# A two-layer encoder trunk on one core: the first projections run while the second half of x is still transposed and split

## What is computed

```python
def rms_norm(x, g):
    y = xf * lax.rsqrt(jnp.mean(xf * xf, axis=-1, keepdims=True) + EPS)
    return y * g
...
h = rms_norm(x, attn_norm_g[0])
qkv = h @ w_qkv                       # 1024 x 3072: q, k, v of 8 heads
q = rms_norm(q, q_g) * (A_HEAD_DIM ** -0.5)
k = rms_norm(k, k_g)
```

## Time and profile before

| | |
|---|---|
| median of 3 runs | 2355.66 us (2349.65 to 2358.06) |
| the profiled execution | 2355.31 us, its span 2353.6 us |
| TensorE busy | 2222.9 us, 94% |
| Vector engine busy | 1593.7 us, 68% |
| Scalar engine busy | 1162.1 us, 49% |
| GpSimd busy | 842.2 us, 36% |
| TensorE busy from 9.1 to 38 us | 15.95 us |
| first projection matmul | at 38.06 us |

### The profile page before, as it was taken

The page is one execution under the profiler, slowest core; times in us unless marked ns, Lnnn a source line. Parts: engine busy times, 40 slices in busy tenths (PEclk is TensorE's granted clock), DMA queues, the critical chain, the costliest instruction groups (busy, mean ns, idle before and its releaser), DMA issues.

```text
span 2353.6 us, 36507 instructions
## 1 busy us (share of the span) xinstructions
PE 2222.9 (94%) x11916; PEld 1909.4 (81%) x11916; DVE 1593.7 (68%) x3173; ACT 1162.1 (49%) x2483; POOL 842.2 (36%) x1464
## 2 busy tenths in 40 slices
PE   6999999976999999899999989998999999899998
PEld 5999999965878888788777988887878888778777
DVE  5688888763576666776776368875576666776773
ACT  4566666653455455533444256653455555543342
POOL 2333333343642222332334155554542233232331
PEclk9999999977999999999999899997999999999999
DMA  6111000002424444762452110003424444663352
GB/s 197 35 28 28 27 27 21 1 19 93 130 82 148 149 153 161 258 241 84 149 197 90 36 37 10 10 19 99 129 87 155 162 158 162 249 223 104 135 173 82
DMA packets 186756, 255.86 MB, mean 109 GB/s; under 512 B 15072, under 2 KB 135904, under 8 KB 181984
## 3 DMA queue, kind: packets, MB, share of 16 engines
q1 hardware_dynamic: 186592, 253.82, 32.3%
HBM read 174.09 MB, written 79.69 MB: 108 GB/s over the span
## 4 chain that ended last, share of the span: by engine, by line
PE 80%; DVE 10%; issue 5%; ACT 3%; DMA 1%; POOLq 1%; POOL 0%; DVEq 0%; SPq 0%; ACTq 0%
PE score L1855 45%; PE trb L1855 13%; PE proj L1855 13%; PE pv L1855 5%; DVE xop L1350 3%; DVE w_op L1350 1%; PE trb L2205 1%; PE trb L1893 1%; ACT p L960 1%; DVE xT L1591 1%; DVE p L1488 1%; DMA w_quad<-in_mlp_w_down 1%; DVE pb L1802 1%; ACT pb L1315 1%; PE trb L1945 0%
## 5 line engine op out<-in xcount | busy, mean ns | idle before, releaser
L1855 PE MATMUL score<-xop,w_op 128*128 128x512 f32 x3840 | 893.8, 392 | 25.3 <-DVE xop L1350 12.6
L1855 PEld LDWEIGHTS score<-xop,w_op 128*128 128x128 f32 x3840 | 720.8, 189 | 185.3 <-issue 36.1
L799 POOL TENSOR_TENSOR w_quad<-w_quad,w_sum 128x512 f32<-128x512 f32 x64 | 99.5, 1555 | 807.1 <-DVE w_op L1350 807.1
L1855 PE MATMUL trb<-xop,w_op 128*128 128x512 f32 x1536 | 361.9, 390 | 5.4 <-DVE w_op L1350 2.0
L1855 PEld LDWEIGHTS trb<-xop,w_op 128*128 128x128 f32 x1536 | 287.4, 188 | 68.8 <-issue 5.8
L923 ACT ACTIVATE w_op<-w_quad 128x512 fp32r<-128x512 f32 (+1 forms) x336 | 216.3, 645 | 247.0 <-PE score L1855 165.3
L1350 DVE TENSOR_TENSOR w_op<-w_quad,w_op 128x512 fp32r<-128x512 f32 (+1 forms) x336 | 285.0, 852 | 43.8 <-ACT w_op L923 43.8
L1591 DVE TENSOR_TENSOR xT<-score,xT 128x512 f32<-128x512 f32 x160 | 109.8, 686 | 159.0 <-PE score L1855 150.9
L1855 PE MATMUL score<-a_hi,w_op 128*128 128x512 f32 x512 | 162.1, 397 | 3.8 <-DVE w_op L1350 3.8
L960 ACT ACTIVATE p<-p,nm_a,slopes 128x128 f32<-128x128 f32 (+7 forms) x124 | 106.6, 861 | 112.6 <-DVE nm_a L1493 110.4
L1350 DVE TENSOR_TENSOR xop<-xop 128x1024 fp32r<-128x1024 f32 x112 | 143.3, 1290 | 16.3 <-ACT xop L923 16.3
(11 more groups left out here) (266 smaller groups left out, 4567.1 us busy)
## 6 DMA issues: line engine op xcount, KB each, us to landing
xop<-u_dram SPq DMA_DIRECT2D x112, 512.0 KB, 5.8
u_dram<-quad SPq DMA_DIRECT2D x32, 1536.0 KB, 9.7
w_quad<-in_mlp_w_up SPq DMA_DIRECT2D x64, 512.0 KB, 5.3
w_quad<-in_mlp_w_down SPq DMA_DIRECT2D x64, 512.0 KB, 4.9
wa_raw<-in_a_w_qkv SPq DMA_DIRECT2D x96, 128.0 KB, 2.4
quad<-xT_dram SPq DMA_DIRECT2D x32, 256.0 KB, 4.2
xT_dram<-xs SPq DMA_DIRECT2D x32, 256.0 KB, 2.6
u_dram<-quad SPq DMA_DIRECT2D x32, 256.0 KB, 4.0
```

Of the source, the lines that this page charges most:

```text
L799: return pool.tensor_tensor(out, x, y, ALU.subtract)
L1855: return nc.tensor.matmul(out, a, b, start=start, stop=stop, **kw)
```

## The change

1. x lies in two buffers of four blocks. The first stands where `v_parts` of both heads will be written, the second and one of the staging buffers in memory that nothing uses in the opening. The staging buffers (four) hold two units each, and one store takes both.
2. SyncE loads the first half of x, then the weights of head 0, then the second half of x. Stores and the loads of the small constants are issued in eight groups.
3. The units 0 to 7 (first half) are worked on with the four quarters of `wa_split` between them. The Scalar engine copies the even units to the staging buffer, the Vector engine the odd ones. The squares are shared: blocks 0, 1, 4, 5 on the Scalar engine, 2, 3, 6, 7 on the Vector engine.
4. The row factors are made by halves (`half_factors`).
5. TensorE runs block 0 as soon as its chunks and weights are there, and then transposes two units of the second half after each of the blocks 0 to 3. These units use two banks; blocks 2 and 3 go into the other two. Block 4 is the first that needs the second half.
6. The small products follow block 5, and only the first scores wait for lambda. The first quarter of the next head's weights is split at block 4 instead of 2.
7. The Scalar engine's function table is loaded by a copy of one column at the start.

```diff
@@ run_heads @@
-            head(-1, 1, False, False, True, True)
+            if first_head:
+                first_head()
+            else:
+                head(-1, 1, False, False, True, True)
@@ helpers @@
+        def x_bank(n):
+            if n < KC:
+                return bank[n % 2][n // 2 % 2]
+            return bank[0][n % 2]
+
         def qkv_bank(h, s):
+            if isinstance(h, int) and h < 0 and s in (2, 3):
+                return bank[1][s - 2]
             return pv if isinstance(h, int) and h < 0 and s % 2 == 0 else proj
@@ SyncE @@
+            load_x(0)
...
             for i in range(4):
                 load_wa(0, i)
+            load_x(1)
-            for n in range(2 * KC):
-                sp.wait_ge(x_staged, n + 1)
...
+            for n in range(0, 2 * KC, 2):
+                sp.wait_ge(x_staged, n // 2 + 1)
+                sp.wait_ge(x_staged_v, n // 2 + 1)
+                sp.dma_start(x_dram[:, n % KC:n % KC + 2, HALF * (n // KC):HALF * (n // KC + 1)],
+                             x_stage[n // 2 % 4][:, :, :]).then_inc(x_stored[n // 2 % 4], 16)
+                for dst, src in small[3 * (n // 2):3 * (n // 2) + 3]:
+                    col(dst, src, const_in)
@@ Scalar engine @@
+            act.wait_ge(made, 2)
+            copy(x_junk[0][:, 0:1], ones[:, 0:1])
+            def x_units(first, end):
+                for n in range(first, end):
+                    half, c = divmod(n, KC)
+                    act.wait_ge(x_tr, n + 1)
+                    copy(a_hi[:, c, HALF * half:HALF * (half + 1)], x_bank(n), gains[:, 0, c:c + 1]).then_inc(x_hi_done, 1)
+                    if n % 2 == 0:
+                        if n >= 8:
+                            act.wait_ge(x_stored[n // 2 % 4], 16)
+                        copy(x_stage[n // 2 % 4][:, 0, :], x_bank(n)).then_inc(x_staged, 1)
+            def first_head():
...
+                for i, (n0, n1) in enumerate(((0, 3), (3, 5), (5, 7), (7, 8))):
+                    x_units(n0, n1)
+                    wa_split(0, True, i, i + 1)
+                x_squares(0)
+                x_squares(1)
+                x_units(8, 12)
+                act.wait_ge(row_stats, 1)
+                step(0)
+                step(1)
+                x_units(12, 14)
+                x_squares(4)
+                x_squares(5)
+                step(2)
+                x_units(14, 16)
+                act.wait_ge(const_in, 16 * CONSTS)
+                act.wait_ge(sinks_done, 1)
+                step(3)
+                act.wait_ge(row_stats, 2)
+                step(4)
+                step(5)
...
@@ Vector engine @@
+            def x_units(first, end):
...
+                    if n % 2:
+                        if n >= 8:
+                            dve.wait_ge(x_stored[n // 2 % 4], 16)
+                        nc.vector.tensor_copy(x_stage[n // 2 % 4][:, 1, :], x_bank(n)).then_inc(x_staged_v, 1)
+                    else:
+                        dve.wait_ge(x_staged, n // 2 + 1)
+                    low(a_lo[:, c, cols], x_bank(n), a_hi[:, c, cols], gains[:, 0, c:c + 1]).then_inc(x_bank_free, 1)
+            def first_head():
...
+                    x_units(n0, n1)
+                    wa_split(0, True, i, i + 1)
+                x_squares(2)
+                x_squares(3)
+                half_factors(0)
+                x_units(8, 12)
+                step(0)
+                step(1)
+                x_units(12, 14)
+                dve.wait_ge(x_half_in[1], 64)
+                x_squares(6)
+                x_squares(7)
+                constants()
+                step(2)
+                x_units(14, 16)
+                step(3)
+                half_factors(1)
+                step(4)
+                step(5)
+                lambdas()
...
@@ TensorE @@
             pe.wait_ge(made2, 1)
+            for n in range(KC):
+                transpose_x(n)
...
-                        elif s >= 2:
-                            pe.wait_ge(qkv_free, s - 1)
-                        elif s == 1:
-
-                            pe.wait_ge(row_stats, 1)
+                        elif s >= 4:
+                            pe.wait_ge(qkv_free, s - 3 if s < 6 else s - 1)
...
+                            if isinstance(h, int) and h < 0 and s in (0, 4):
+                                pe.wait_ge(x_bank_free, 2 * s + k + 1)
...
-                        if isinstance(h, int) and h < 0 and s == 0:
+                        if isinstance(h, int) and h < 0 and s < 4:
+                            transpose_x(KC + 2 * s)
+                            transpose_x(KC + 2 * s + 1)
+                        if isinstance(h, int) and h < 0 and s == 5:
                             small_products()
```

More of the change, by code:

```diff
@@ new lines, in x_squares, with step @@
+            def x_squares(b):
+                nc.scalar.activation(x_junk[0][:, :], x_tok[b // 4][:, b % 4, :], ACT.Square,
+                                     accum_out=msq[:, b:b + 1]).then_inc(x_squared, 1)
+                act.drain()
+            def first_head():
+                def step(s):
+                    head(-1, 1, False, False, True, True, (s,))
+                act.wait_ge(gain_in, 16)
+                for i, (n0, n1) in enumerate(((0, 3), (3, 5), (5, 7), (7, 8))):
[18 more added lines that the diff above has]
+                step(5)
+                act.wait_ge(small_mm, 1)
+                nc.scalar.activation(lam_e[:, :], score[0][:, 0:2], ACT.Exp).then_inc(lam_exp, 1)
+                step(6)
+                step(7)
+                for i in range(4):
+                    act.wait_ge(x_stored[i], 2 * 16)
@@ L1014, in high_early, with head @@
                 copy(a_hi[:, c, :], oT[:, c, :]).then_inc(o_early_hi, 1)
-            def head(h, par, attn, tail, qkv, more):
+            def head(h, par, attn, tail, qkv, more, steps=range(NB)):
                 uses = uses_a(h, attn, tail, qkv)
-                for s in range(NB):
+                for s in steps:
                     t = h * NB + s
@@ L1052, in head @@
                         high_pair(uses, h, s, par)
-                    if s == 2 and more:
+                    if s == (2 if attn else 4) and more:
                         wa_split(h + 2, par == 0, 0, 1)
@@ new lines, in lambdas, with step @@
+            def lambdas():
+                dve.wait_ge(lam_exp, 1)
+                nc.vector.tensor_copy(sinks[:, :], score[0][:, 16:32])
+                nc.vector.tensor_tensor(neg_lam[:, :], lam_e[:, 1:2], lam_e[:, 0:1], ALU.subtract)
+                dve.drain()
+                nc.vector.tensor_scalar(neg_lam[:, :], neg_lam[:, :], -LAM0, None, ALU.add)
+                dve.drain().then_inc(row_stats, 1)
+            def first_head():
+                def step(s):
+                    head(-1, 1, False, False, True, True, (s,))
+                dve.wait_ge(gain_in, 16)
+                for i, (n0, n1) in enumerate(((0, 3), (3, 5), (5, 7), (7, 8))):
+                    x_units(n0, n1)
[18 more added lines that the diff above has]
+                lambdas()
+                step(6)
+                step(7)
+                for i in range(4):
+                    dve.wait_ge(x_stored[i], 2 * 16)
+                dve.wait_ge(made3, 1)
@@ L1861, in three, with transpose_x @@
                 return mm(out, a[1], b[0], False, stop, **kw)
-            pe.wait_ge(made2, 1)
-            for n in range(2 * KC):
+            def transpose_x(n):
                 half, c = divmod(n, KC)
```

145 lines of the change are left out of this document (69 added, 76 removed).

## The result

| | before | changed |
|---|---|---|
| median of the runs | 2356.52 us (2349.65 to 2358.66, 6 runs) | 2339.66 us (2336.36 to 2341.84, 6 runs) |
| the profiled execution | 2355.31 us, span 2353.6 | 2336.36 us, span 2334.6 |
| TensorE busy | 2222.9 us | 2213.6 us |
| Scalar / Vector / GpSimd busy | 1162.1 / 1593.7 / 842.2 us | 1162.6 / 1595.2 / 844.4 us |
| first projection matmul | 38.06 us | 17.41 us |

The ratio is 0.9932, with a 95% interval of 0.992 to 0.9945: the changed kernel is 13 to 19 us faster, a gain of 0.7%. The busy times of three engines are the same to 2.2 us, so no work went away; TensorE's fell by 9 us. The mark stands 83.33 - 69.46 = 13.87 us earlier.

What follows compares the result with a forecast made beforehand. TensorE bounds the kernel, so the opening pays only where it idles or runs slow: the second head's block 0 ends at 71.0 instead of 83.5 us, 12.5 us less, 2355.3 - 12.5 = 2342.8 us; range 2338 to 2351.

Steps and rivals of the forecast that it cites:

- mark: Last matmul of the second head's block 0, at 83.33 us before; forecast at 71.0 with clock's fall and handovers.
- waits before units 10, 11: TensorE between blocks 1 and 2: waits 0.6 us for unit 10's bank and 0.8 for unit 11's.
- first pair: First q/k transposes, before block 4: GpSimd done at 42.7 us, TensorE waits about 0.9 us.
- second pair: Second q/k transposes, before block 6: GpSimd done at 54.2 us, TensorE waits 1.9 us.
- block 7 to the mark: From block 7's end in the first head to block 0's end in the second: 6.40 us, unchanged.
- clock's fall, handovers: Half speed for 2.7 us after the 1.9 us wait, +1.3 us; handovers the sum leaves out, +0.3 us.
- The copy's 0.60 us: Vector engine's copy of x out of PSUM, start to start, from a similar instruction's row; ends 0.48 and 0.75.
- The rivals: Clock at 1.2 GHz until block 4 (chance 0.11), x late (0.05), head start given back (0.04), slower (0.03).
- first rival: TensorE stays at 1.2 GHz until block 4: price 7.5 us, 2350 us; chance 0.11.
- 1.28 us on the path, gone: Scalar engine's table load moves to an idle time before 9 us, saving 1.28 us.
- 3.70 us, gone, hidden behind the first projections: Scalar engine's wait for a store of x: staging buffers hold two units, none reused before unit 8.
- The prediction is the shift of that 83.33: Gain equals how much earlier the second head's block 0 ends; nothing behind it touches the instruction streams.

Runs made afterwards that it cites:

- c_serial: Changed kernel with all 16 units transposed ahead of block 0, none between blocks: 2342.28 us median, ratio 0.994 to the kernel before.
- c_pool: Changed kernel with the squares of blocks 6 and 7 on the Scalar engine instead of the Vector engine: 2341.63 us.
- c_both: Changed kernel with units 8 and 9 before the first row factors and squares 6 and 7 on the Scalar engine: 2341.88 us, ratio 0.9938 to the kernel before.
- c_units_first: Changed kernel with the Vector engine taking units 8 and 9 before its first chain of row factors: 2338.47 us.
- c_act_copies: Changed kernel with every plain copy of x on the Scalar engine, none on the Vector engine: 2338.56 us.
- b_table: Kernel before with the Scalar engine's function table loaded by a one-column copy at the start: 2356.26 us.
- b_staging: Kernel before with eight staging buffers of one unit in place of four: 2349.32 us.
- the second pair of traces: Both kernels run once more unaltered: changed kernel 2337.41 us, kernel before 2351.59 us.
- c_late_table: Changed kernel without the early table load, so the table is loaded before the first `hi`: 2346.93 us.

## Why the prediction was right

2342.8 us was forecast and 2339.66 measured, inside the range; the gain of 12.5 us was measured as 13.87 and 14.34 at the mark. Step by step:

| step | forecast | measured |
|---|---|---|
| first projection | 17 to 18 | 17.41 |
| Vector engine done with the first half | 22.9 | 22.07 + 0.95 = 23.0 |
| block 0 ends | 24.2 | 24.24 |
| waits before units 10, 11 | 0.6, 0.8 | 1.06, 0.60 |
| first pair: wait, start | 0.9, 42.95 | 2.27, 44.82 |
| second pair: wait, start | 1.9, 54.25 | none, 54.36 |
| block 7 ends | 63.0 | 63.04 |
| block 7 to the mark | 6.40 | 6.42 |
| clock's fall, handovers | +1.3, +0.3 | none, none to be seen |
| mark | 71.0 | 69.46 |

**What held.** The copy's 0.60 us was the nearest row's, and exact. The Trainium skill (VectorE: DVE Perf Modes, "Why PSUM operands drop a tier"), which the forecast weighed, gives an fp32 operand in PSUM no doubled rate. The trace agrees: the copy out of PSUM has a 0.68 us record beside the 0.69 of the earlier trace rows. The second half of x caused no wait: c_serial shows it there at 19.76 us, forecast near 21. The weights of the second head were in time, and the 6.4 us between block 7 and the mark stayed. The rivals are out: blocks 1 to 3 ran with matmuls 0.17 apart, unit 8 didn't wait for DMA, and nothing was given back.

**Two errors that cancelled, by luck.** The first pair was forecast at a wait of 0.9 us and had 2.27; its transposes began at 44.82, where GpSimd was to be done at 42.7. Two steps failed. "Block 1's statistics leave the Vector engine at about 36.0" was 0.8 short: they left at 36.80. And "GpSimd takes 6.7 us" was 1.3 short: from 36.80 to the transposes it is 8.0. Undisturbed the chain takes 6.0 (c_pool, c_both), but here it took 44.82 - 36.89 = 7.9, since the change puts two squares of the Vector engine beside it. The 6.7 us had the same thing in it once, as rows of the kernel before show, GpSimd's and the Vector engine's:

```profile
56.71 0.84 POOL L459 TENSOR_TENSOR chain_p<-chain_p 128x8 f32<-128x8 f32 x1
```

```profile
56.53 0.96 DVE L1350 TENSOR_TENSOR wa_lo<-wa_raw,wa_hi 128x768 fp32r<-128x768 f32 x1
```

The instruction took 0.84 in place of 0.20 us and ended at 57.55, the split of the weights beside it at 57.49. The second pair was forecast at 1.9 and had none: its chain was done at 52.70 + 1.05 = 53.75, not at 54.2, and TensorE came later than forecast, with the first wait behind it. The sum of the two, 2.8 against 2.27, hardly shows it; block 7's end is right to 0.2 us for that reason (63.0 was an end, 63.04 is the start of the last matmul, and the next instruction starts at 63.22). A forecast of a sum of waits that hang on each other is better than one of its parts, as c_units_first and c_pool show from the other side: a wait taken away at one place was there again at the next.

**The clock.** "The 1.9 us wait may do the same, for 2.7 us at half speed: +1.3. I put it in": in both traces of the changed kernel the waits of 2.27 and 2.57 us were followed by a granted clock of 1.00. The 1.9 us wait itself wasn't there. In c_act_copies (2.76 us of wait) and c_units_first (4.26) the clock fell, and cost 2.4 and 1.5 us. The Trainium skill (TensorE: Matmul & The Clock Gate, "HAM oscillation — how this bites in real kernels"), which the forecast named for its first rival, has a clock halved again after a pause; those two traces agree, and in the changed kernel nothing of the kind is seen. With the 1.3 out, and the 0.3 of handovers, the sum gives 69.4 for the end of the block, which was at 69.6. This term was the main error of the 12.5.

**A reading that was too simple.** "1.28 us on the path, gone" and "3.70 us, gone, hidden behind the first projections" were added up as parts of one way. As single edits of the kernel before they are worth nothing (b_table) and 1.9 us (b_staging); together they won 3.56 us at the first projection, and in the one execution there is, with a late constant and a fall of the clock, nothing at the mark. They count in full only with row factors that no longer stand behind the constants. The forecast's sum is right because it was built as a new timeline from 11.6 us on, and not from these differences.

**What was beyond it.** "The prediction is the shift of that 83.33" comes out for the second pair of traces to 0.2 us, in the sum alone, and misses 5 us of the first. The median came out 3.1 us under the forecast, 1.4 to 1.8 of it in the opening. The rest lies behind the mark, where the forecast had put nothing, and where both the spread of executions and the sliding-window attention's 2.6 to 3.1 us are larger than it.

## What to carry to other kernels

A gain in an opening is read at a mark behind which all streams are the same, since the stages behind it differed by 4.5 us between two executions of one kernel; and even a stretch that the change doesn't touch should be compared over several traces of both kernels. Price a restructured opening as a new timeline for each engine, with the waits in it as one chain: an edit that removes one wait is worth only the distance to the next thing that is late, here the small constants and the row factors behind them before the change, and block 1's statistics after it. Before putting work with two inputs in SBUF on the Vector engine, look at what GpSimd does in those microseconds.

## What the runs showed that was not expected

- Two GpSimd instructions on 128x8 took 1.09 and 1.22 us in place of 0.20 and 0.24, each to within 0.1 us of the end of a 128x1024 square on the Vector engine; without the squares (c_pool) both were short. It goes the other way too: in c_act_copies a Vector instruction of 0.23 us, at 43.74, took 0.98 beside GpSimd's product. Vector instructions that read PSUM did no harm in the changed kernel: the chain's rows at 39.28 and 39.64 kept their 0.20 and 0.24 us beside a copy (39.06) and a split (39.65). The Trainium skill (SBUF — State Buffer, "SBUF: two separate sides") says that the two engines' shared ports are an exclusive lock for a whole instruction, which a Vector operation with two inputs in SBUF takes against a GpSimd operation that reads SBUF. The trace agrees: the short ones ended with the long ones, and were not just slower.
- A wait of TensorE of 2.27, 2.49 or 2.57 us wasn't followed by the clock's lower level (1.2 GHz), one of 2.76 was, and so was one of 1.34 in c_late_table and one of 2.53 in the earlier trace rows. The waits before units 10 and 11 are 1.08 and 0.60 us in c_late_table and 1.06 and 0.60 in the changed kernel, and only in c_late_table did the clock fall behind them: the length of the wait alone doesn't tell.
- The twelve weight loads were issued in 7.31 us with four large loads before them and 10.33 with eight.
